# A second place for rotary tiles, a third bank for attention values, and attention steps dealt by estimated TensorE work

## What is computed

```python
def hybrid_layer(x, mem, ...):
    h = rms_norm(x, ln_g)
    u = einsum('bsd,de->bse', h, w_in)            # q, k, v, z of four branches, forget logits, 4 x 1024 gate logits
    o_sb = stick_breaking_attention(q_sb, k_sb, v_sb)                     # 4 heads
    o_fx = forgetting_attention(rms_norm(q_fx), rms_norm(k_fx), v_fx, log_sigmoid(f_fx + b))
    o_dl = dilated_mixture(rope(rms_norm(q_dl)), rope(rms_norm(k_dl)), v_dl)   # 12 heads in 3 dilation groups
    km, vm = split(rms_norm(mem) @ w_mem_kv)
    o_mm = memory_cross_attention(rms_norm(q_mm), rms_norm(km), vm)
    y = [(o * silu(z)) @ w_br for each branch]
    g = sigmoid(gate_logits)
    return x + (sum of g[b] * y[b]) @ w_out
```

## Time and profile before

| | |
|---|---|
| median of 3 executions | 1451.46 us (1451.34 to 1453.76) |
| the profiled execution | 1452.88 us |
| its span, first to last instruction | 1451.1 us |
| mean granted TensorE clock | 0.971 of full |
| TensorE busy | 1352.4 us (93%) |
| GpSimd busy | 687.0 us (47%) |
| ScalarE busy | 664.3 us (46%) |
| VectorE busy | 485.3 us (33%) |
| mean DMA rate | 83 GB/s |

### The profile page before, as it was taken

The page is one execution under the profiler, slowest core; times in us unless marked ns, Lnnn a source line. Parts: engine busy times, 40 slices in busy tenths (PEclk is TensorE's granted clock), DMA queues, the critical chain, the costliest instruction groups (busy, mean ns, idle before and its releaser), DMA issues.

```text
span 1451.1 us, 17623 instructions
## 1 busy us (share of the span) xinstructions
PE 1352.4 (93%) x6234; PEld 1048.6 (72%) x6234; DVE 485.3 (33%) x765; ACT 664.3 (46%) x1233; POOL 687.0 (47%) x571
## 2 busy tenths in 40 slices
PE   7987999998899999999998789999889999999998
PEld 5655878765667688888876578778656677888876
DVE  3456240234422122223335553213433312222231
ACT  5334422367444454544444434225664445454441
POOL 3445631244323267767545566213432423776762
PEclk9998999999999999999999999999999999999999
DMA  7443331121222134434354334112122221444442
GB/s 214 122 102 94 88 73 37 37 51 44 52 50 59 44 96 109 115 100 117 98 156 120 95 88 109 30 31 51 44 51 52 52 64 50 108 113 105 106 116 87
DMA packets 210031, 120.78 MB, mean 83 GB/s; under 512 B 9752, under 2 KB 200472, under 8 KB 209944
## 3 DMA queue, kind: packets, MB, share of 16 engines
q1 hardware_dynamic: 209944, 119.66, 31.7%
HBM read 107.04 MB, written 6.29 MB: 78 GB/s over the span
## 4 chain that ended last, share of the span: by engine, by line
PE 74%; DVE 9%; ACT 7%; POOL 5%; issue 4%; DMA 1%; SPq 0%; DVEq 0%; ACTq 0%; POOLq 0%
PE dense L728 56%; PE score L728 9%; PE acc L728 3%; PE out L728 3%; POOL normed L1646 2%; POOL w_lo L1601 2%; ACT w_hi L1145 1%; DVE turned L1467 1%; DVE normed L1456 1%; PE turn L728 1%; DVE negmax L1509 1%; DVE raw L1409 1%; DVE probs L1467 1%; PE turn L863 1%; ACT dq_hi L1221 1%
## 5 line engine op out<-in xcount | busy, mean ns | idle before, releaser
L1601 POOL TENSOR_TENSOR w_lo<-w_raw,w_hi 128x512 fp32r<-128x512 f32 (+1 forms) x404 | 489.0, 1216 | 671.9 <-ACT w_hi L1145 627.1
L728 PE MATMUL dense<-h_hi,w_hi 128*128 128x512 f32 x1168 | 511.2, 438 | 25.5 <-DVE raw L1409 20.7
L728 PE MATMUL dense<-h_lo,w_hi 128*128 128x512 f32 x1168 | 467.2, 400 | 0.0
L728 PE MATMUL dense<-h_hi,w_lo 128*128 128x512 f32 x1168 | 466.7, 400 | 0.0
L728 PEld LDWEIGHTS dense<-h_hi,w_hi 128*128 128x128 f32 x1168 | 226.3, 194 | 98.8 <-DVE raw L1409 26.8
L728 PEld LDWEIGHTS dense<-h_lo,w_hi 128*128 128x128 f32 x1168 | 226.6, 194 | 54.3 <-issue 14.2
L1145 ACT ACTIVATE w_hi<-w_raw 128x512 fp32r<-128x512 f32 (+1 forms) x401 | 232.7, 584 | 66.4 <-PE dense L728 64.1
L728 PEld LDWEIGHTS dense<-h_hi,w_lo 128*128 128x128 f32 x1168 | 225.6, 193 | 50.6
L1407 DVE TENSOR_TENSOR sig<-dense,x_rstd_row 128x512 f32<-128x512 f32 x48 | 33.2, 692 | 212.0 <-issue 122.7
L1409 DVE TENSOR_TENSOR raw<-dense,x_rstd_row 128x512 f32<-128x512 f32 x80 | 55.1, 688 | 136.4 <-PE dense L728 107.9
L1198 ACT ACTIVATE sig<-sig 128x512 f32<-128x512 f32 x48 | 30.3, 632 | 125.9 <-DVE sig L1407 125.9
(11 more groups left out here) (252 smaller groups left out, 1901.4 us busy)
## 6 DMA issues: line engine op xcount, KB each, us to landing
w_raw<-in_w_in SPq DMA_DIRECT2D x292, 256.0 KB, 2.9
w_raw<-in_w_out SPq DMA_DIRECT2D x32, 256.0 KB, 2.8
x_scratch<-v_dil SPq DMA_DIRECT2D x16, 256.0 KB, 3.5
w_raw<-in_w_mem_kv SPq DMA_DIRECT2D x16, 256.0 KB, 2.8
v_dil<-x_scratch SPq DMA_DIRECT2D x16, 256.0 KB, 2.8
turned<-normed SPq DMA_DIRECT2D x48, 64.0 KB, 2.0
probs<-normed SPq DMA_DIRECT2D x48, 64.0 KB, 2.0
silu_z<-in_mem SPq DMA_DIRECT2D x4, 512.0 KB
```

The source lines that it names most:

```text
L728: return nc.tensor.matmul(o, lhsT, rhs, start=start, stop=stop, skip_group_check=True)
L1601: pool.tensor_tensor(w_lo[:, g % SPLIT_SLOTS, c], w_raw[:, g % RAW_SLOTS, c], f(w_hi[:, g % SPLIT_SLOTS, c]), ALU.subtract).then_inc(w_lo_ ...
```

## The change

- **Rotary places.** Two `normed` (the second is `o_norm`), two `turned` (the second is `inv_den`), and the cosine product goes to `probs` slots 1 and 2 at post3, as soon as `normed` is there. post4 (sine product and sum) stands at a tile's end behind post1, post5 in the middle of the next one. Ring waits are kept for each place.
- **Head sums and transposes** of dilated tiles and memory's keys and values alternate between bank T and A1.
- **Value banks.** `OUT_BANK` gives heads one of three banks, O, A0, A1.
- **Dealing.** `tensor_work` estimates each step's TensorE work, and `dense` deals so that the work given is in proportion to the dense steps done. `inv` and `fin2` are issued two at a time.
- **Lag and rooms.** lag=2 for the value tiles and memory tiles; five rooms before memory's steps.
- **The start.** Two low parts of the first half come before the second half's copies, the rest interleaved with those of the second half, each half with a semaphore of its own; two of ScalarE's squares and the splits change order.

```diff
+OUT_BANK = {DIL: (0, 1, 2, 0), MM: (0, 1, 2, 0), FOX: (1, 2, 0, 1)}
...
-            if later:
+            for _ in range(min(2, len(later))):
                 yield later.pop(0)
...
+    def tensor_work(step):
+
+        kind = step[0]
+        if kind in ("row", "col"):
+            b, h, c = step[1:]
+            if h % 2 == 0:
+                return 0
+            width = S - c * P if b == FOX else S
+            if kind == "row":
+                return {DIL: 2200, MM: 1200, FOX: 2600}[b]
+            return 700 + {DIL: 5000 if c >= 2 else 3500, MM: 2600, FOX: 5 * width + 2 * P}[b]
+        if kind == "pv":
+            return {DIL: 1950, MM: 1950, FOX: 4 * (S - step[3] * P)}[step[1]]
+        if kind in ("sb_z", "sb_sum", "sb_pv"):
+            p, j, e = step[1:]
+            width = S - j * P
+            return {"sb_z": (700 + 4 * width) * e, "sb_sum": 100 + 2 * width, "sb_pv": 2 * width * (j > 0) + 4 * width * e}[kind]
+        return {"max": 1200, "room": 700, "x_sum": 700, "mem_t": 700, "mem_square": 700, "mem_scale": 700}.get(kind, 0)
...
-        done = given = 0
+        done = given = spent = 0
+        work = sum(map(tensor_work, others))
...
-            while given * places < len(others) * done:
+            while given < len(others) and (done == places or spent * places < work * done):
+                spent += tensor_work(others[given])
                 steps.append(others[given])
                 given += 1
...
             if h == 0:
-                for r in waiting[4]:
-                    add("post4", r)
-                waiting[5] += waiting[4]
-                waiting[4] = []
+                for r in waiting[5]:
+                    add("post5", r)
...
                 for r in waiting[3]:
                     add("post3", r)
-                for r in waiting[5]:
-                    add("post5", r)
-                waiting[5] = []
-                waiting[4] += [r for r in waiting[3] if r.rope]
+                for r in waiting[4]:
+                    add("post4", r)
+                waiting[5] = waiting[4]
+                waiting[4] = [r for r in waiting[3] if r.rope]
                 waiting[3] = []
                 waiting[2].append(t)
...
-          [("mem_square",), ("mem_scale",)] + [("mem_t", c) for c in range(4)])
-    dense(pair_of("mk", MM) + pair_of("mv", MM))
+          [("room",)] * 5 + [("mem_square",), ("mem_scale",)] + [("mem_t", c) for c in range(4)], lag=2)
+    dense(pair_of("mk", MM) + pair_of("mv", MM), lag=2)
...
-        turned_of = [turned[:, :], probs[:, P_SLOTS - 1, :]]
+        normed_of = [normed[:, :], o_norm[:, :]]
+        turned_of = [turned[:, :], inv_den[:, :]]
...
+                i = rope_tiles.index(s[1].n) % 2 if s[1].rope else 0
+                normed_users[i].append((s[1].n, rope_done if s[1].rope else qk_lo_ready, s[1].n))
                 if s[1].rope:
-                    (turned_users, spare_users)[rope_tiles.index(s[1].n) % 2].append((s[1].n, qk_lo_ready, s[1].n))
+                    turned_users[i].append((s[1].n, qk_lo_ready, s[1].n))
...
+        in_other_bank = set([t.n for t in tiles if t.n in head_summed.n or t.n in v_turned.n
+                             if t.branch == DIL or t.kind in ("mk", "mv")][1::2])
...
+        def turn_place(t):
+
+            return A1 if t.n in in_other_bank else T
+
+        def turn_place_free(t):
+            return (out_ring[2] if t.n in in_other_bank else turn_ring).before(t.n)
+
+        def rope_place(t):
+            return rope_tiles.index(t.n) % 2 if t.rope else 0
+
+        def normed_place(t):
+            return normed_of[rope_place(t)]
+
+        def cosine_place(t):
+            return probs[:, 1 + rope_place(t), :]
+
         def turned_place(t):
-
-            return turned_of[rope_tiles.index(t.n) % 2] if t.rope else turned[:, :]
+            return turned_of[rope_place(t)]
 
...
-                            sp.dma_start(turned_of[i][32 * q:32 * q + 32, :], normed[32 * (q ^ 1):32 * (q ^ 1) + 32, :])\
+                            sp.dma_start(turned_of[i][32 * q:32 * q + 32, :], normed_of[i][32 * (q ^ 1):32 * (q ^ 1) + 32, :])\
...
-                        once((first_h_lo, KT + kt + 1))
+                        once((first_h_lo[0], kt + 1))
+                        once((first_h_lo[1], kt + 1))
...
-                        ob = (O, A0)[h % 2]
+                        ob = (O, A0, A1)[OUT_BANK[b][h]]
...
             first_square(0)
+            first_square(1)
             first_split(0)
-            first_square(1)
             act.wait_ge(params_in, 16 * DEPTH)
             first_high(0)
-            first_square(2)
             first_split(1)
             first_high(1)
+            first_square(2)
+            first_split(2)
             first_square(3)
-            first_split(2)
             act.wait_ge(setup, 2)
...
+            def x_place(i):
+                for a in range(2):
+                    dve.wait_ge(x_turned, 2 * i + a + 1)
+                    dve.tensor_copy(xT[:, 4 * a:4 * a + 4, i * P:(i + 1) * P],
+                                    turn_bank(i, a)[:, :].rearrange("p (k s) -> p k s", k=4)).then_inc(x_placed, 1)
+
+            def first_low(u, kt):
                 c = slice(u * MEM, (u + 1) * MEM)
-                for kt in range(KT):
-                    dve.wait_ge(first_h_hi, u * KT + kt + 1)
-                    dve.scalar_tensor_tensor(out=h_lo[:, kt, c], in0=xT[:, kt, c], scalar=ln_all[:, kt:kt + 1],
-                                             in1=f(h_hi[:, kt, c]), op0=ALU.mult, op1=ALU.subtract).then_inc(first_h_lo, 1)
+                dve.wait_ge(first_h_hi, u * KT + kt + 1)
+                dve.scalar_tensor_tensor(out=h_lo[:, kt, c], in0=xT[:, kt, c], scalar=ln_all[:, kt:kt + 1],
+                                         in1=f(h_hi[:, kt, c]), op0=ALU.mult, op1=ALU.subtract).then_inc(first_h_lo[u], 1)
+
+            x_place(0)
+            x_place(1)
+            dve.wait_ge(x_placed, 4)
+            dve.wait_ge(params_in, 16 * DEPTH)
+            first_low(0, 0)
+            first_low(0, 1)
+            x_place(2)
+            x_place(3)
+            dve.wait_ge(x_placed, 8)
...
-                        dve.tensor_tensor(swapped, normed[:, :], swapped, ALU.add).then_inc(rope_done.sem, 1)
+                        dve.tensor_tensor(swapped, cosine_place(t), swapped, ALU.add).then_inc(rope_done.sem, 1)
...
-                    elif kind == "post4":
-                        t = s[1]
-                        pool.wait_ge(*halves_there(t))
-                        pool.tensor_tensor(normed[:, :], normed[:, :], rope[:, 0, :], ALU.mult).then_inc(cos_done.sem, 1)
+                    elif kind == "post3" and s[1].rope:
+                        t = s[1]
+                        pool.wait_ge(*normed_ready.of(t.n))
+                        pool.tensor_tensor(cosine_place(t), normed_place(t), rope[:, 0, :], ALU.mult).then_inc(cos_done.sem, 1)
```

More of the change, by code:

```diff
@@ L849, in _ @@
                         once((const_in, 16 * CONST_LOADS))
[L850 removed]
+                        wait(pe, turn_place_free(t))
                         pe.wait_ge(*squared.of(t.n))
[L852 removed]
+                        mm(turn_place(t)[:, 0:t.width], headsum[:, :], square[:, square_ring.slot(t.n), 0:t.width], start=True, stop=True)\
                             .then_inc(head_summed.sem, 1)
```

66 lines of the change are left out of this document (30 added, 36 removed).

## The result

The changed kernel takes 1405.0 us (median; 1403.9 to 1406.2) beside 1452.4 us of the kernel before on the same chip: a ratio of 0.9673, 95% interval 0.9657 to 0.9690, 47 us faster. 1378 was forecast, with a range of 1352 to 1408. The profiled execution took 1405.65 us, its span 1403.9. The range holds the time; the forecast's own range (1366 to 1392) does not, and 26 of the 73 us are missing.

What follows compares the result with a forecast made beforehand. A chain of waits across engines was taken to bound the rotary tiles; other stages have different limits. Gains of 57.4 + 5.6 + 8 + 2 + 0 = 73.0 us gave 1378 us, range 1352 to 1408.

Steps and rivals of the forecast that it cites:

- rotary tile period of 7.5 us: Rival: a chain survives in the rotary tiles; 28.6 us gained there instead of 57.4, 1407 us in all; chance 0.11.
- Part 1: Rotary tiles: breaking the loop across engines brings twelve tiles to 6.3 us each, gaining 57.4 us (47.8 to 67.0).
- (a): Rotary tiles: TensorE next in line, 5.43 us of dense matmuls plus 0.45 for the head sum, 5.9 a tile.
- three limits near 5.9: Rotary tiles: TensorE 5.9 us, VectorE and GpSimd obstructing each other 5.5 (6.7 with full durations), remaining chain 5.9.
- three causes of the loop: Rotary tiles: post4 before post2 in VectorE's queue, only one `normed`, and cosine product ahead of low weights in GpSimd's queue.
- port rival: Rotary tiles: VectorE and GpSimd take turns for whole instructions, 6.7 us a tile, 9.6 us less gain, 1388; chance 0.17.
- Part 2: Attention steps dealt by work: dilated 114.9 us, stick-breaking 68, rest 4.5; gain 2.8 us a layer, 5.6 together.
- stick-breaking too dense: Rival: ScalarE, VectorE and TensorE queues lock step; stick-breaking 80 us for 68, 24 us lost, 1402; chance 0.14.
- Part 3: Three value banks and earlier finishes: fewer TensorE waits in memory and forgetting; 4 us a layer, 8 us (bounds 0, 8.3 a layer).
- Part 4: Start: second half's low parts and copies come earlier, so dense work starts sooner; 2 us gained, bounds 0 and 2.4.
- Part 5: Value and memory tiles: lag 2, five rooms, later transposes with about 1 us slack; gain 0, bounds 3 either way.
- What would show it: Signs include rotary evacuations 6.3 us apart, stick-breaking about 68 us, ScalarE over 70% busy there, first dense matmul near 15.7.

Runs made afterwards that it cites:

- rotary part alone: Kernel before with only two places, early cosine product, later low parts and alternating head sums; start, lags, rooms, banks, finishes and dealing as before: 1403.7 us.
- x2.2 kernel: Changed kernel with the planner's figures for stick-breaking steps times 2.2: 1384.4 us, ratio 0.955.
- kernel by number with memory early: Changed kernel with steps dealt by number, and value and memory tiles dealt as before (lag 1, no empty rooms, early memory transposes): 1381.3 us, ratio 0.953.

## Why the range held and the terms were wrong

The range of 1352 to 1408 holds 1405.0 because it was stretched to the slow rivals, and none of them came as described: no rotary tile period of 7.5 us, no stick-breaking of 80. That it holds is luck in part. Side by side, from the medians (us; gains positive), each as the difference of two kernels that differ in it alone, save for banks and finishes. "Start" is 1407.6 - 1405.0, "dealing" 1388.6 - 1405.0, "value and memory" 1381.3 - 1388.6, "rotary" 1451.0 - 1403.7, "banks and finishes" 1408.4 - 1388.6, by the correction above. Since the parts act on each other, another order of undoing them would share the sum differently:

| term | forecast | by experiments |
|---|---|---|
| rotary | 57.4 | 47.2 |
| dealing by work | 5.6 | -16.5 |
| banks and finishes | 8 | 19.8 |
| start | 2 | 2.6 |
| value and memory | 0 | -7.3 |
| sum | 73.0 | 45.8 (measured 47.4) |

**Part 1, rotary: the mechanism right, size 10 too large.** The loop is broken, and the limit that I named as (a), TensorE, is the one that holds, but at 6.35 us a tile and not 5.9, since the head sum costs 0.86 and not 0.45 (and 24 dense matmuls 5.49, not 5.43). My 6.3 was a margin over three limits near 5.9 and met the true one by luck; 75.6 against 75.8 us in the table of stretches is the sum of that luck and of the value group's lag and rooms. I counted twelve tiles at 6.3, and three of them are value tiles; in the rotary part alone v dil 0 and v dil 1 take 7.4 and 8.2, 3 us more together. That kernel gains 50.9 us in the rotary stretches and 47.2 in all. Of the three causes of the loop that I named, only the order was taken back by itself (0.8 us a tile); the other two, with the second head-sum bank, are 1.6 together.

**The port rival (1388) is out, but not for want of mutual delay.** From q dil 2 to k dil 5 nine rotary tiles take 57.8 and 57.4 us, 6.4 each, and TensorE's period is 6.35; five evacuations in a row come 6.14 to 6.15 apart, catching up behind one of 7.41. All this is under the 6.7 to which whole durations sum. By the rule of the Trainium skill ("SBUF — State Buffer", section "SBUF: two separate sides"), the ports that VectorE and GpSimd share are an exclusive lock, held for the whole instruction by a GpSimd instruction or by one of VectorE's with two SBUF inputs. The trace agrees with it but for 0.14 us. All through layer two's rotary stretch a VectorE instruction of this kind that overlaps one of GpSimd's ends 0.55 us behind it (0.69 alone), and a held-up GpSimd instruction ends 1.13 to 1.16 us behind VectorE's (1.28 alone). In the lines above the sine product ends at 771.01, the cosine product at 772.14, the sum at 772.68, the low weights at 773.84. The evacuation, which reads a bank, keeps its 0.69 beside GpSimd. So a tile needs 4 x 0.55 + 3 x 1.15 = 5.7 us of these ports, near the 5.5 that I had read, and TensorE's 6.35 stays above it. The rival was wrong in its price: whole durations count about 0.14 us too much for each instruction that was held up.

**Part 2, dealing: this is the step that failed.** I took TensorE's own work of stick-breaking, 57.0, times the 1.15 of today, plus 2.3. The pieces are near: dilated 114.7 for 114.9, stick-breaking 70.3 for 68, the rest of k fox 1 7.4 for 4.5; together 192.4 for 187.4. The steps fell as I had counted (233 and 100 dense matmuls, 9.7 and 4.2 tiles for 9.75 and 4.5). The ratio of 1.15 that I kept is the failed step: it became 70.3 / 56.5 = 1.24. With it I booked each dense tile taken away from stick-breaking as a saving of 5.43 x 1.15 = 6.2 us. And I compared with a stretch of before that was itself lengthened by the bank waits. The x2.2 kernel measures their true price: 66 matmuls there, the work of 2.75 tiles, cost 5.2 us, 1.9 for each 24, because they fill waits for ScalarE and GpSimd, and the granted clock is 0.93 instead of 0.88. Moved among dilated steps, where TensorE is busy 96.5%, they cost 5.5 for each 24. I had no term for a change of the clock in these stages, and by the accounting above slower matmuls are 14.7 of the 19.8 us that the dealing by work costs. The rival "stick-breaking too dense" (0.14, 24 us lost, 1402) is nearest: the engines do wait for each other there, and 20.6 us come back when it is undone. But its stretch of 80 us did not come; stick-breaking takes 70.3, and the loss lies in dense work dealt to the wrong stretch and in the slower matmuls that went with it.

**Part 3, banks and finishes: right place, under half of the size.** I counted the 5.4 us of one stage and nothing in the dilated stage, though its third and fourth heads use the same banks. Before, TensorE waited there too, from 186 to 285 us:

```profile
PE acc L728 <- DVE o_norm L1549: 1.6, 1, 1.6
```

The rotary part alone and the kernel by number with memory early differ only in the start and in banks and finishes. Their dilated and stick-breaking stretches are 190.2 / 190.4 and 185.1 / 188.1 us, memory and forgetting 147.0 and 139.9: 5.1 and 2.3, and 7.1 a layer. Of the 7.1, 4.8 us are idle time, the wait that I had named, and 2.3 are matmuls at a granted clock of 1.00 instead of 0.99. The second is near my bound of 8.3; the first I had at nothing. In the changed kernel this gain is there but the dealing takes it back: its 4.4 us a layer are 7.1 less 2.7. My agreement with the table (4 for 4.4) was again a sum of two errors.

**Part 4, start: right**, 2.6 for 2 (bound 2.4).

**Part 5, value and memory: wrong.** "About 1 us of slack" was read for the transposes' reader; the wait is in another resource, the two slots of `raw`, which a lag of 2 holds a tile longer. I had bounded it at 3 us over both layers; it is 7.3 (lags and rooms together). The code shows two slots and the release at the silu, so the evacuation of mk 0 was there to be followed.

**What would show it.** Seen as named: granted clock 1.0 in rotary, rotary sums no longer behind their own cosine product, no wait for `o_norm`, ScalarE over 70% busy in stick-breaking (50.75 of 70.3), first dense matmul at 15.46 for 15.7. Rotary evacuations are 6.3 us apart only on average (6.1 to 7.4). Not seen: 68 us for stick-breaking (70.3).

## What to carry to other kernels

Deal filler work to the stage whose engines wait, not in proportion to the bounding engine's own work: a planner that counts only TensorE needs a weight for branches that run as a chain (here 2.2 times, 20.6 us). Read the busy time of equal matmuls beside the idle time: most of what a bad deal cost here stood in slower matmuls. Before crediting an edit with a wait that it removes, look for the other edits of the same change that remove it too: bank and finishes were worth 20.5 and 11.8 us alone and 19.8 together. And a stretch that comes out as forecast confirms no term while several edits act in it; two of mine agreed here by errors that cancelled.

## What the runs showed of the hardware

- A head sum between dense matmuls costs TensorE 0.86 us: 0.46 for its two matmuls and 0.40 on the second dense matmul behind them (0.63 instead of 0.23).
- Time at TensorE's lower level after the first dense matmul was 2.7, 5.7 and 6.1 us in three profiles and none in a fourth, and does not follow the order of work ahead of it: two kernels with the same order have 2.7 and 6.1, two others none and 5.7.
- The same 890 matmuls of the dilated and stick-breaking stretch were 174.6 us of busy time with stick-breaking at a granted clock of 0.88, and 170.1 at 0.93; the idle time fell with it, from 17.8 to 12.1 us. In memory and forgetting, 2.3 us of idle time in 7 were followed by 7 us at 0.71, and 1.4 in 7 by none below 1.00.
- A VectorE instruction with two SBUF inputs (0.69 us alone) and one of GpSimd's (1.28 alone) take turns: the one held up ends 0.55 or 1.13 to 1.16 us behind the other, 0.14 sooner than if whole instructions excluded each other. VectorE's evacuation of a bank is not held up (0.69).
